# A two-block transformer kernel on one core: lead counted in projection chunks, variance sums inside a key tile, a values chunk ahead of the scores, gate input copied before key rotation

## What is computed

```python
def first_block(x, ...):
    h = rms_norm(x, mix_norm_g)
    q, kv, gate_logits, conv_in = split(h @ w_in)
    attn = nsa_attention(q, kv, sigmoid(gate_logits), rel_bias, cmp_pos, cmp_w1, cmp_w2)
    conv = silu(layer_norm(causal_depthwise_conv(a * sigmoid(gate), conv_w, conv_b)))
    x = x + concat(attn, conv) @ w_out
    h = rms_norm(x, ffn_norm_g)
    u = causal_depthwise_conv(h @ w_up, cw, cb)       # 3 taps, 2 x 5632 columns
    x = x + (silu(gate_of(u)) * a_of(u)) @ w_down
    return rms_norm(x, final_norm_g)

def second_block(x, c, positions, ...):
    shift_m, scale_m, gate_m, shift_f, scale_f, gate_f = split(silu(c) @ w_ada + b_ada)
    z = (rms_norm_2(x) * (1 + scale_m) + shift_m) @ w_in_2
    c_q, c_kv, k_rope, q_g, k_g, v_g, a_g, r_g = split_cols(z)
    o = concat(mla_mixer(c_q, c_kv, k_rope, ...), gla_mixer(q_g, k_g, v_g, a_g, r_g, ...)) @ w_out_2
    x = x + gate_m * rms_norm_2(o)
    h = rms_norm_2(x) * (1 + scale_f) + shift_f
    return x + gate_f * rms_norm_2((silu(h @ w_ffn_gate) * (h @ w_ffn_up)) @ w_ffn_down)
```

## Time and profile before

| what | value |
|---|---|
| runs | 2320.01, 2320.11, 2322.33 us; median 2320.11 |
| the profiled execution | 2319.82 us, of it 2317.7 us span from first to last instruction |
| PE busy | 2248.6 us (97%) |
| DVE busy | 1626.9 us (70%) |
| ACT busy | 1122.9 us (48%) |
| POOL busy | 22.1 us (1%) |
| DMA | 498.89 MB, mean 215 GB/s |
| mean granted TensorE clock | 0.988 |
| the chain that ended last | PE 91%, DVE 5%, ACT 2% |

### The profile page before, as it was taken

How to read it: one execution, slowest core, us unless ns; L and a number is a source line. 1 busy time by engine, 2 the same in 40 slices (tenths; PEclk the granted TensorE clock), 3 DMA queues, 4 the chain that set the end, 5 groups by cost and what they waited for, 6 DMA issues and landing times.

```text
span 2317.7 us, 30876 instructions
## 1 busy us (share of the span) xinstructions
PE 2248.6 (97%) x12330; PEld 1911.4 (82%) x12330; DVE 1626.9 (70%) x2291; ACT 1122.9 (48%) x1689; POOL 22.1 (1%) x51
## 2 busy tenths in 40 slices
PE   7999999999999999999999999989999999999997
PEld 7999777888888888887879786777888888888886
DVE  6998886889887798897775555557555555554554
ACT  5433774555553355554455565445444344344443
POOL 1000000000000000000000001000000000000000
PEclk9999999999999999999999999999999999999999
DMA  8654435688888888888765552446666677655553
GB/s 266 214 166 134 136 99 201 207 275 284 272 312 322 284 280 274 271 281 288 293 223 199 164 182 64 128 140 214 234 228 223 212 241 235 210 188 189 187 182 109
DMA packets 137406, 498.89 MB, mean 215 GB/s; under 512 B 15440, under 2 KB 15584, under 8 KB 137008
## 3 DMA queue, kind: packets, MB, share of 16 engines
q1 hardware_dynamic: 136512, 494.44, 63.3%
q0 software_dynamic: 752, 2.49, 0.6%
HBM read 494.38 MB, written 2.49 MB: 214 GB/s over the span
## 4 chain that ended last, share of the span: by engine, by line
PE 91%; DVE 5%; ACT 2%; issue 1%; POOL 0%; DMA 0%; SPq 0%; DVEq 0%; ACTq 0%
PE bank L611 38%; PE both L611 26%; PE bank L603 20%; DVE w_lo L1596 1%; PE bank L574 1%; DVE conv_y L1705 1%; ACT w_hi L1137 1%; PE bank L821 1%; PE both L782 1%; PE bank L803 1%; PE bank L1096 0%; PE bank L658 0%; ACT junk L1150 0%; DVE ada_acc L1580 0%; DVE x L2217 0%
## 5 line engine op out<-in xcount | busy, mean ns | idle before, releaser
L1596 DVE TENSOR_TENSOR w_lo<-raw,w_hi 128x1024 fp32r<-128x1024 f32 x737 | 890.6, 1220 | 452.9 <-ACT w_hi L1137 451.3
L1137 ACT ACTIVATE w_hi<-raw 128x1024 fp32r<-128x1024 f32 x737 | 763.5, 1053 | 644.2 <-PE bank L611 364.3
L603 PE MATMUL bank<-h_both,w_hi 128*128 128x512 f32 x1408 | 494.8, 400 | 6.6 <-DVE w_lo L1596 6.6
L603 PE MATMUL bank<-h_both,w_lo 128*128 128x256 f32 x1408 | 381.5, 281 | 0.0
L603 PEld LDWEIGHTS bank<-h_both,w_hi 128*128 128x128 f32 x1408 | 259.6, 188 | 64.7 <-DVE w_lo L1596 8.8
L611 PE MATMUL both<-w_hi,h_both 128*128 128x512 f32 (+1 forms) x960 | 296.3, 384 | 3.3 <-DVE h_both L1667 2.0
L611 PE MATMUL bank<-w_hi,h_both 128*128 128x512 f32 (+2 forms) x1024 | 298.0, 372 | 0.0
L603 PEld LDWEIGHTS bank<-h_both,w_lo 128*128 128x128 f32 x1408 | 266.4, 189 | 8.3
L611 PE MATMUL bank<-h_both,w_hi 128*128 128x256 f32 (+1 forms) x1312 | 244.0, 288 | 1.8 <-DVE w_lo L1596 1.1
L1580 DVE SCALAR_TENSOR_TENSOR ada_acc<-raw,stat,ada_acc 128x1024 f32<-128x1024 f32 x180 | 230.1, 1278 | 0.2
L611 PEld LDWEIGHTS bank<-w_hi,h_both 128*128 128x128 f32 x1024 | 187.3, 188 | 33.4 <-issue 0.7
(11 more groups left out here) (357 smaller groups left out, 2629.9 us busy)
## 6 DMA issues: line engine op xcount, KB each, us to landing
raw<-weights SPq DMA_DIRECT2D x924, 512.0 KB, 4.4
raw<-weights SPq DMA_DIRECT2D x5, 504.0 KB, 3.6
x<-x SPq DMA_DIRECT2D x2, 1024.0 KB, 5.7
bias<-bias_rows POOLq DMA_DIRECT2D x8, 256.0 KB, 11.8
out<-x SPq DMA_DIRECT2D x8, 256.0 KB, 2.2
phase<-params SPq DMA_DIRECT2D x1, 497.0 KB, 10.5
raw<-weights SPq DMA_DIRECT2D x1, 488.0 KB, 3.3
lasting<-params SPq DMA_DIRECT2D x1, 478.0 KB, 9.7
```

The source lines that it names most:

```text
L603: t = e.matmul(into, s, a, start=opening, stop=closing)
L1137: e.activation(w_hi[:, n % PART_SLOTS, 0:widths[i]], raw[:, i % RAW_SLOTS, 0:widths[i]], ACT.Copy).then_inc(hi_ready, 1)
L1596: e.tensor_tensor(w_lo[:, slot, 0:widths[i]], raw[:, i % RAW_SLOTS, 0:widths[i]], w_hi[:, slot, 0:widths[i]].bitcast(F32), ALU.subtract).t ...
```

## The change

`lead(i)` replaces `i + AHEAD`: it is the third chunk after i that is no ada chunk. It stands in nearly all calls of `round_until` and `rests_until`, in `made` among them. PE's sums of squares move from behind key tile (1,1) into key tile (2,0), behind its first chunk; values step 1 moves ahead of the scores of unit 0; `unit_output(0)` moves behind `unit_transpose(1)`. The gate input is transposed behind the third `gla_k` tile and copied by DVE ahead of `rotate_keys`. No operation is added or left out, nothing moves on POOL or SP.

```diff
+        def lead(i):
+            return ([j for j in range(i + 1, len(kinds)) if kinds[j] != "ada"][AHEAD - 1:] or [len(kinds)])[0]
...
             for at_key, (br, j) in enumerate(((1, 1), (2, 0), (2, 1))):
-                tile(("key", br, j), h_hi, h_lo, need, (keys_ready, at_key + 2))
-                if at_key == 0:
+                steps = tile_steps(("key", br, j), h_hi, h_lo, need)
+                if at_key == 1:
+                    next(steps)
                     fill(7)
-                    for j in range(CONV_TILES):
-                        w.wait_ge(squared, j + 1)
-                        t = e.matmul(banks[7][:, 0:T], ones, ln_sq[:, j, :], start=j == 0, stop=j == CONV_TILES - 1)
+                    for i in range(CONV_TILES):
+                        w.wait_ge(squared, i + 1)
+                        t = e.matmul(banks[7][:, 0:T], ones, ln_sq[:, i, :], start=i == 0, stop=i == CONV_TILES - 1)
                     t.then_inc(ln_varied, 1)
                     free[7] = ln_var_ready, 1
+                whole(steps)
+                free[bank_of["key", br, j]] = keys_ready, at_key + 2
...
             out_project(0)
+            out_project(1)
             for v in range(NV + 3):
                 if v < NV:
                     unit_scores(v)
-                if v >= 3:
+                if v > 3:
                     unit_output(v - 3)
                 if 2 <= v < NV + 2:
                     unit_transpose(v - 2)
+                if v == 3:
+                    unit_output(0)
                 for step in out_steps(v):
-                    if step:
+                    if step > 1:
                         out_project(step)
...
                 turn_latents(WITH_GLA_K[h])
-            fill(6)
-            for tt in range(TT):
-                t = e.transpose(banks[6][0:GATE_RANK, tt * P:(tt + 1) * P], c_kv[:, tt, KV_RANK + ROPE:], identity)
-            t.then_inc(a_lr_turned, 1)
-            free[6] = a_lr_ready, 1
+                if h == 2:
+                    fill(6)
+                    for tt in range(TT):
+                        t = e.transpose(banks[6][0:GATE_RANK, tt * P:(tt + 1) * P], c_kv[:, tt, KV_RANK + ROPE:], identity)
+                    t.then_inc(a_lr_turned, 1)
+                    free[6] = a_lr_ready, 1
...
             def made(key):
-                round_until(final[key] + AHEAD)
+                round_until(lead(final[key]))
...
             def made(key):
-                rests_until(final[key] + AHEAD)
+                rests_until(lead(final[key]))
...
+            w.wait_ge(a_lr_turned, 1)
+            e.tensor_copy(a_lr[:, :], banks[6][0:GATE_RANK, 0:T]).then_inc(a_lr_ready, 1)
             for _ in rotate_keys():
                 pass
-            w.wait_ge(a_lr_turned, 1)
-            e.tensor_copy(a_lr[:, :], banks[6][0:GATE_RANK, 0:T]).then_inc(a_lr_ready, 1)
```

More of the change, by code:

```diff
@@ L1220, in scalar_program @@
                 e.activation(gates[:, tt, :, :].rearrange("p h b -> p (h b)"), banks[2 + tt][:, 0:NG], ACT.Copy).then_inc(gates_ready, 1)
-            round_until(final["key", 1, 1] + AHEAD)
+            round_until(lead(final["key", 1, 1]))
             flat = cmp_p[:, :, :].rearrange("p u n -> p (u n)")
@@ L1234, in scalar_program @@
                 if at_key == 0:
-                    round_until(final["key", 2, 0] + AHEAD)
+                    round_until(lead(final["key", 2, 0]))
                     w.wait_ge(ln_var_ready, 1)
@@ L1287, in scalar_program @@
             for n in range(4):
-                round_until(final["out_attn", n] + AHEAD)
+                round_until(lead(final["out_attn", n]))
                 for tt in range(TT):
@@ L1328, in scalar_program @@
                 for n in range(4):
-                    round_until(final["down1", half, n] + AHEAD)
+                    round_until(lead(final["down1", half, n]))
                     if half:
@@ L1402, in scalar_program @@
                 for piece in range(1, 14, 2):
-                    round_until(groups[key][piece][0] + AHEAD)
+                    round_until(lead(groups[key][piece][0]))
                     if at_group < 3:
@@ L1772, in vector_program @@
             e.tensor_tensor(cmp_p[:, :, :], cmp_p[:, :, :], cmp_max.unsqueeze(2).to_broadcast([P, NU, NCMP]), ALU.subtract).then_inc(cmp_shifted, 1)
-            rests_until(final["key", 1, 0] + AHEAD)
+            rests_until(lead(final["key", 1, 0]))
             w.wait_ge(ln_mean_ready, 1)
@@ L1777, in vector_program @@
                 e.tensor_tensor(conv_y[:, j, :], conv_y[:, j, :], ln_mean[:, :], ALU.subtract).then_inc(centred, 1)
-            rests_until(final["key", 1, 1] + AHEAD)
+            rests_until(lead(final["key", 1, 1]))
             w.wait_ge(cmp_exped, 1)
@@ L1794, in vector_program @@
             e.tensor_scalar(v, banks[7][:, 0:T], 1.0 / CONV_CH, EPS, ALU.mult, ALU.add).then_inc(ln_var_ready, 1)
-            rests_until(final["key", 2, 0] + AHEAD)
+            rests_until(lead(final["key", 2, 0]))
             w.wait_ge(ln_root, 1)
@@ L1806, in vector_program @@
                 e.tensor_tensor(conv_y[:, j, :], conv_y[:, j, :], r, ALU.mult).then_inc(ln_scaled, 1)
-            rests_until(final["key", 2, 1] + AHEAD)
+            rests_until(lead(final["key", 2, 1]))
             for j in range(CONV_TILES):
@@ L1924, in vector_program @@
                         diagonals(0, param("final_norm_g"), (2, 3))
-                        rests_until(groups[key][11][0] + AHEAD)
+                        rests_until(lead(groups[key][11][0]))
                         normed(0, x)
@@ L2099, in vector_program @@
                 for piece in range(1, 14, 2):
-                    rests_until(groups[key][piece][0] + AHEAD)
+                    rests_until(lead(groups[key][piece][0]))
                     if at_group < 3:
@@ L2105, in vector_program @@
                 if at_group == 2:
-                    rests_until(final[key] + AHEAD)
+                    rests_until(lead(final[key]))
                     for _ in decaying:
                         pass
-            rests_until(final["gla_r", 1] + AHEAD)
+            rests_until(lead(final["gla_r", 1]))
             for i in range(2):
@@ L2278, in vector_program @@
                         ff_rest(g - 1, groups["gate", g][0][0])
-                    rests_until(final["gate", g] + AHEAD)
+                    rests_until(lead(final["gate", g]))
                     outs = made(("up", g))
@@ L2353, in gpsimd_program @@
                 e.dma_start(bias[at_row:P:apart, :, :], along).then_inc(bias_landed, 16)
-            rests_until(final["out_attn", 3] + AHEAD)
+            rests_until(lead(final["out_attn", 3]))
             norm_power(out1_factor, out1_total, 1.0 / D, 1)
```

52 lines of the change are left out of this document (26 added, 26 removed).

## The result

The changed kernel took 2300.61 us in the median of 4 runs (2297.6 to 2302.31), the kernel before 2320.22 beside it: a ratio of 0.9912, 95% interval 0.9895 to 0.9929. Faster by 16 to 24 us, against a forecast of 2302 in 2297 to 2310. The profiled execution took 2299.26 us, its span 2297.2, which is 20.5 less than the span before.

The account below looks back on a forecast made before the run. PE, busy 97% of the span, was taken as the bound, so only its waits and slow-clock stretches could pay. Terms summed to 18.4 us, less 0.4 gave 18.0; from 2319.82 that leaves 2301.8, stated as 2302 us, range 2297 to 2310.

Parts of the forecast that it names:

- The lead, 5.7 us: Up projection: a third prepared chunk cuts PE's w_lo waits from 6.6 to 0.9 us; bounds 3 and 6.6.
- just in time with no room: Start of up projection: DVE runs without room after making h, so 0.9 us of the wait at 460.86 stays.
- The last up tile, 3.5 + 1.4: Before the second down projection: 3.5 us from PE's wait, 1.4 from the slow clock behind it (bounds 0 and 1.4).
- Squares, keys and values, 1.9: Attention: 0.8 us by the scores of unit 0 and the 1.1 us values wait gone; bounds 0.7 and 4.
- End of the first block, 0.7: PE's 0.83 us wait for h_both shrinks, 0.7 us gained; bounds 1 us lost and 1.2 gained.
- Gate input, 2.4 + 2.8: At the gate matmul: 2.4 of PE's 2.5 us wait, plus 2.8 from the slow clock behind it (bounds 0 and 3.3).
- the clock does not follow: Rival, chance 0.20: the 1.4 + 2.8 = 4.2 us from slow stretches is not gained; 2306.2 us.
- It has 0.06 us in a tile to spare: Up projection: DVE's assumed room per tile, from its 1.7 us join wait against PE's 1.68 us column sums.
- two rivals: DVE as the up projection's bound (0.14, 2307.7 us) and slower, DVE idling before w_lo in 84 tiles (0.03, e.g. 2331).
- DVE is the bound: Rival, chance 0.14: in the up projection all six waits come back at other tiles, 5.7 us lost; 2307.7 us.
- 0.4 that I had taken off for nothing: First tiles of the up projection: 0.4 us deducted for small waits where DVE makes it by only 0.1 us.

Follow-up runs that it names:

- the gate input alone: Kernel before with only the gate input's transposes behind the third key head and its copy ahead of the key rotation; 2316.35 us, ratio 0.9979.
- the key tiles alone: Kernel before with only variance sums inside key tile (2,0), second values chunk and first unit output moved; 2315.97 us, ratio 0.9985; repeated 2316.04, 0.9986.
- the lead alone: Kernel before with only the new lead count, used everywhere; key tiles, values and gate input as before; 2305.11 us, ratio 0.993.

## Why the prediction was right, and where its terms were off

**The lead, 5.7 us: right, and the cause with it.** All five waits of about 1 us fell as forecast. At the start I kept 0.9 us at 460 and 0.36 stayed, so the waits gave 6.2. DVE was not "just in time with no room" there: it had the room described below.

**The last up tile, 3.5 + 1.4: right.** From the first matmul of the second down projection to the column sums in it PE took 16.3 us before (1046.72 to 1063.01) and 10.9 in the changed kernel (1037.82 to 1048.71): 5.4, where I had 4.9. The four other waits between 460.86 and 1186.03 are 4.0 together, and this stretch is 10.6 shorter; 1.2 us remain unassigned, 0.6 among the up tiles ahead of the last and 0.5 behind the column sums.

**Squares, keys and values, 1.9: right in kind, 1.3 to 1.4 measured.** The new wait came at 242.57 with 2.20 us (forecast 242.2, 2.1), the squares' wait is 1.5, the values' wait is gone. The 0.7 us earlier arrival was seen at the end of that wait; about 0.5 of the 1.9 was lost behind it.

**End of the first block, 0.7: right in size.** PE's wait for h_both went from 0.83 to 0.24.

**Gate input, 2.4 + 2.8: right in these runs, by luck in part.** 2.3 and 3.0 with the gate input alone. But the second term is the price of a slow stretch, and the key tiles alone lost the same stretch with the wait in place. With the key tiles alone 1.8 of the 3.0 came back as a slow stretch behind the next wait. The rival "the clock does not follow" had the right doubt and, for this kernel, the wrong outcome. The Trainium skill, "TensorE: Matmul & The Clock Gate", Part 1, says that how many matmuls run cold depends on the run. The traces of one kernel agree at 204 us (granted clock 0.52 in one profile of before, 1.00 in the other). At the gate matmul the two profiles of a kernel were alike (103.29 and 103.32 us to the next landmark before, 100.33 and 100.32 with the key tiles alone), and the spans behind the same 2.52 us pause differed between kernels with equal work there: 103.29, 101.90 and 100.33.

**"It has 0.06 us in a tile to spare": wrong.** This was the step under two rivals. I had set DVE's longest wait for a join (1.7 us) against the 1.68 us of PE's column sums, as if DVE could only be idle at its joins. It was idle 0.38 us ahead of a tile's taps, waiting for ACT, in the kernel before (430 to 645 us) as in the changed one; an added addition of 0.4 us went into that gap at no cost, and about 0.6 us in all are there. The rival "DVE is the bound" deserved less than the 0.14 it had. The list that the earlier trace rows is taken from has these two lines as well:

```profile
DVE ffn_a L1877 <- ACT ffn_a L1319: 7.5, 19, 0.4
DVE ffn_g L1877 <- ACT ffn_g L1325: 6.4, 19, 0.3
```

**What the sum missed.** 18.0 forecast, 20.5 in the profile. The 2.5 between them: 0.5 from the smaller remainder at 460, 0.5 from the last tile, the 1.2 unassigned, 1.0 from a shorter slow stretch at the start of the up projection, which was no term at all and is luck of the profiled run (54.29 us, where the same kernel took 55.53 in its second profile, and the lead alone 55.51, with nearly the same waits), 0.4 that I had taken off for nothing, less 0.6 at the key tiles and 0.5 in all the rest. The parts alone come to 15.7 + 4.6 + 3.6 = 23.9 us and the whole to 20.4 and 20.9 in its two sessions: they do not add up. That each takes some slow stretches with it that another takes too would explain it, and the table bears it out for one: the key tiles alone and the gate input alone each shorten the stretch behind the gate matmul by 3.0 us, which can be gained once.

## What to carry to other kernels

A lead counted in positions of a queue is as long as the work between them: where a stream mixes chunks that the consumer waits for with others, count only the first kind. Take an engine's room from all its waits in a stage, not from the one that looks like the last, and if it matters, measure it by adding an operation, then two. When runs of one kernel scatter by 5 us of 2300, with a lower granted clock in the longer ones, judge a change of 2 us by distances between landmarks of the trace, and leave the clock term as a range. Look behind the next wait as well before a lost slow stretch is booked as gain.

## What was not expected of the hardware

A pause of PE of 2.52 us, the same in all, was followed by a stretch partly at 1.2 GHz in two executions of before (0.69 and 0.74 over 1282 to 1293) and by full clock in two executions of a kernel that differs 1000 us earlier (1.00 and 1.00). It cost 3.0 us with the stretch and nothing without, but without it a stretch of 7 us behind the next pause (1.28 us) had 0.76 and 1.8 us went there. Both outcomes repeated for their kernel in two profiles each, which is too few to exclude scatter; what sets it is open. And a slow stretch came with no pause at all: at 204 us, after 24 us of busy PE, in one of two executions of the same kernel.
